# DeltaNet beside a streamed projection: keys turned one window ahead, key and query products as two jobs, TensorE's jobs placed by token half

## What is computed

```python
q, k, v = split(silu(causal_depthwise_conv(qkv, conv_w)))      # 4 taps
q, k = l2_normalize(heads(q)), l2_normalize(heads(k))
...
a_low = where(strict, einsum(k_beta, k) * gamma, 0)            # 64 x 64, per chunk of 64 tokens
u, w = triangular_solve(a_low + eye, [v * beta, k_beta * exp(decay)])
qk = einsum(q, k) * gamma
def step(state, inp):                                          # over the four chunks
    v_new = u_n - w_n @ state
    o_n = q_n @ state + qk_n @ v_new
    state = state * d_n + k_n.T @ v_new
o = rms_norm(o, norm_g) * silu(heads(z))
```

## Time and profile before

| | |
|---|---|
| median of 3 runs | 1931.12 us (1929.06 to 1935.96) |
| the profiled execution | 1928.9 us, its span 1927.1 us |
| granted TensorE clock, mean | 0.993 |
| busy: PE, PEld | 1875.4 us (97%), 1544.2 us (80%) |
| busy: DVE, ACT, POOL | 1100.5 (57%), 886.7 (46%), 130.9 us (7%) |
| DVE's split L1020, 584 times | 727.1 us, mean 1247 ns |
| ACT's split L673, 584 times | 618.8 us, mean 1061 ns |
| DMA | 316.37 MB, mean 164 GB/s |

### The profile page before, as it was taken

How to read it: one execution, slowest core, us unless ns; L and a number is a source line. 1 busy time by engine, 2 the same in 40 slices (tenths; PEclk the granted TensorE clock), 3 DMA queues, 4 the chain that set the end, 5 groups by cost and what they waited for, 6 DMA issues and landing times.

```text
span 1927.1 us, 29055 instructions
## 1 busy us (share of the span) xinstructions
PE 1875.4 (97%) x10770; PEld 1544.2 (80%) x10770; DVE 1100.5 (57%) x1441; ACT 886.7 (46%) x1384; POOL 130.9 (7%) x90
## 2 busy tenths in 40 slices
PE   7998998998999999999999999999999999999998
PEld 6877877877877888888888888888888888888886
DVE  5466576676676656666555555555544445555454
ACT  5453354353354355555444444444433344444443
POOL 0023023023023000000000000000000000000010
PEclk9999999999999999999999999999999999999999
DMA  7543333333333354444466655555555555555554
GB/s 255 173 143 115 116 121 121 110 123 118 111 121 121 110 170 141 153 152 141 163 196 199 205 197 208 186 185 177 191 191 193 196 186 188 185 185 193 191 193 142
DMA packets 88018, 316.37 MB, mean 164 GB/s; under 512 B 9712, under 2 KB 10224, under 8 KB 87792
## 3 DMA queue, kind: packets, MB, share of 16 engines
q1 hardware_dynamic: 87056, 312.65, 49.1%
q0 software_dynamic: 576, 2.10, 0.3%
q10 hardware_dynamic: 288, 0.18, 0.0%
HBM read 312.79 MB, written 2.10 MB: 163 GB/s over the span
## 4 chain that ended last, share of the span: by engine, by line
PE 89%; POOL 3%; DVE 3%; issue 3%; ACT 1%; DMA 0%; DVEq 0%; ACTq 0%; POOLq 0%; SPq 0%
PE acc L275 26%; PE acc L276 25%; PE acc L277 25%; PE J L398 4%; PE J L330 2%; PE J L446 1%; POOL rg L1455 1%; PE J L437 1%; PE J L454 1%; DVE cT L1075 1%; DVE qn L1075 1%; ACT w_hi L673 1%; PE J L489 1%; PE J L318 0%; POOL mats L1477 0%
## 5 line engine op out<-in xcount | busy, mean ns | idle before, releaser
L1020 DVE TENSOR_TENSOR w_lo<-raw,w_hi 128x1024 fp32r<-128x1024 f32 x584 | 727.1, 1247 | 635.2 <-ACT w_hi L673 633.6
L673 ACT ACTIVATE w_hi<-raw 128x1024 fp32r<-128x1024 f32 x584 | 618.8, 1061 | 684.2 <-PE acc L277 681.5
L275 PE MATMUL acc<-w_hi,hT_hi 128*128 128x512 f32 x1440 | 581.9, 404 | 8.4 <-DVE hT_lo L1038 4.3
L276 PE MATMUL acc<-w_lo,hT_hi 128*128 128x512 f32 x1440 | 564.2, 392 | 0.0
L277 PE MATMUL acc<-w_hi,hT_lo 128*128 128x512 f32 x1440 | 564.2, 392 | 0.0
L275 PEld LDWEIGHTS acc<-w_hi,hT_hi 128*128 128x128 f32 x1440 | 272.0, 189 | 71.2 <-issue 7.6
L277 PEld LDWEIGHTS acc<-w_hi,hT_lo 128*128 128x128 f32 x1440 | 272.0, 189 | 58.6
L276 PEld LDWEIGHTS acc<-w_lo,hT_hi 128*128 128x128 f32 x1440 | 272.5, 189 | 52.5 <-issue 1.0
L275 PE MATMUL acc<-w_hi,act_hi 128*128 128x512 f32 x512 | 199.3, 389 | 0.0
L277 PE MATMUL acc<-w_hi,act_lo 128*128 128x512 f32 x512 | 199.2, 389 | 0.0
L276 PE MATMUL acc<-w_lo,act_hi 128*128 128x512 f32 x512 | 199.2, 389 | 0.0
(11 more groups left out here) (224 smaller groups left out, 1498.4 us busy)
## 6 DMA issues: line engine op xcount, KB each, us to landing
raw<-weights SPq DMA_DIRECT2D x584, 512.0 KB, 3.3
xres<-x SPq DMA_DIRECT2D x4, 512.0 KB, 7.3
xres<-x POOLq DMA_DIRECT2D x4, 512.0 KB, 5.7
y<-nat SPq DMA_DIRECT2D x8, 256.0 KB, 3.1
fgain_sb<-fgain SPq DMA_DIRECT2D x1, 1024.0 KB, 6.9
masks_sb<-masks SPq DMA_DIRECT2D x1, 640.0 KB, 10.7
zs<-w_ba SPq DMA_DIRECT2D x1, 256.0 KB, 9.2
dist_sb<-dist SPq DMA_DIRECT2D x1, 192.0 KB, 3.5
```

Source lines behind the costliest of these rows:

```text
L275: mm(o, aT_hi[:, kt, tok], w_hi[:, c % RING, w], start=first, stop=False)
L276: mm(o, aT_hi[:, kt, tok], w_lo[:, c % RING, w], start=False, stop=False)
L673: A(w_hi[:, slot], raw[:, slot], ACT.Copy).then_inc(hi_ready, 1)
L1020: tt(w_lo[:, slot], raw[:, slot], w_hi[:, slot].bitcast(F32), ALU.subtract).then_inc(lo_ready, 1)
```

## The change

On PE the jobs are called after each token half's triple of products (`fine`), at places s = 0 to 127, with a table of its own; ACT and DVE keep 64 places with a table each. Raw K is turned 12 places before its window's end (`k_step`, called with s - 128 and h - 64 for the next group), and ACT's copies and the first tap follow there. Decay rows come before Q's front. Q's silu is written straight to `kq`, unnormalised, so that normalised Q isn't turned; Q's sum of squares enters as a term of the output's norm (`nq_done`). Key by key and key by query are two jobs (`inner`), at places 30 and 46. DVE makes the first X and U of the key product and ready masks; POOL makes those masks earlier. Z is not turned: its rows are evacuated with the two chunks of a tile exchanged, its silu is taken on them, and DVE's final scale takes it in (eight operations). After OT, ACT and DVE write `og_hi` and `og_lo` straight from PSUM. The diff, cut to its core:

```diff
-FRONT = {ITEM_K: 0, ITEM_Q: 1, ITEM_V: 25, ITEM_Z: 37}
-BANK = {ITEM_K: 0, ITEM_Q: 2, ITEM_V: 2, ITEM_Z: 2}
-TAPS = {ITEM_K: (0, 1, 2), ITEM_Q: (3, 5, 7), ITEM_V: (26, 28, 31)}
-TANH = {ITEM_K: 3, ITEM_Q: 9, ITEM_V: 32}
-SILU = {ITEM_K: 4, ITEM_Q: 10, ITEM_V: 33}
-BACK = {ITEM_K: 10, ITEM_Q: 16, ITEM_V: 34}
-NORM = {ITEM_K: 13, ITEM_Q: 19}
-ROWS, TK, TQ, KKQ, INV, QTM, OT = 11, 16, 21, 22, 25, 40, 63
-P1, P2, P3 = (40, 45, 50, 55), (42, 47, 52, 57), (44, 49, 54, None)
+BANK = {ITEM_K: 0, ITEM_Q: 2, ITEM_V: 2}
+PE_FRONT = {ITEM_K: -12, ITEM_Q: 19, ITEM_V: 56}
+PE_BACK = {ITEM_K: 16, ITEM_Q: 50, ITEM_V: 73}
+PE_ROWS, PE_TK, PE_KK, PE_KQ, PE_QT, PE_OT = 11, 28, 30, 46, 76, 126
+PE_INV_V = (46, 50, 55, 60, 69)
+PE_INV_U = (49, 52, 56, 66, 71)
+PE_P1, PE_P2, PE_P3 = (76, 85, 98, 109), (78, 92, 101, 112), (82, 96, 107, None)
+ACT_CONV = {ITEM_K: -4, ITEM_Q: 8, ITEM_V: 31}
+ACT_TANH = {ITEM_K: 5, ITEM_Q: 16, ITEM_V: 33}
+ACT_NSQ = {ITEM_K: 7, ITEM_Q: 27}
+ACT_EXP, ACT_NORM, ACT_KQ, ACT_Z, ACT_QT, ACT_OT = 6, 8, 13, 35, 38, 63
+ACT_INV = (21, 22, 27, 31, 33)
+ACT_VO = (40, 47, 49, 56)
+ACT_OSQ = (48, 59)
+DVE_CW, DVE_PAR = -17, 0
+DVE_TAPS = {ITEM_K: (-3, 0, 0), ITEM_Q: (8, 8, 16), ITEM_V: (31, 31, 31)}
+DVE_SILU = {ITEM_K: 5, ITEM_Q: 16, ITEM_V: 33}
+DVE_ROWS, DVE_NK, DVE_KQ, DVE_KK, DVE_EYE, DVE_KQM, DVE_NQ, DVE_VB, DVE_Z = 4, 7, 11, 14, 17, 19, 22, 35, 38
+DVE_INV = (21, 21, 24, 31, 34)
+DVE_RH, DVE_O, DVE_S = (37, 41, 49, 52), (38, 45, 49, 56), (38, 47, 52, None)
+DVE_OSUM, DVE_OSCALE, DVE_OT = 59, 59, 63
+STEPS, HALVES = 64, 128
...
                     for k in range(CK):
                         for t in range(NT):
                             last = product(par, t, aT_hi, aT_lo, c, k, c == 0 and k == 0, c == nch - 1 and k == CK - 1)
-                        if k == CK - 1:
-                            last.then_inc(chunk_used, 1)
+                            if k == CK - 1 and t == NT - 1:
+                                last.then_inc(chunk_used, 1)
+                            if fine:
+                                fine(NT * (h0 + c * CK + k) + t)
...
-            def gdn_step(h, g):
-                for n in range(4):
-                    if h == FRONT[n]:
-                        pe.wait_ge(rawg_a, 4 * g + (n + 1))
-                        if n == ITEM_K:
-                            pe.wait_ge(og_f, 2 * g + 2)
-                        if n == ITEM_V:
-                            pe.wait_ge(at_ready, g + 1)
-                        if n == ITEM_Z:
-                            pe.wait_ge(vb_done, g + 1)
-                        turn_group(rawg[:, n], BANK[n], front_T)
-                for n in (ITEM_K, ITEM_Q, ITEM_V):
-                    if h == BACK[n]:
-                        pe.wait_ge(silu_done, 4 * g + (n + 1))
-                        if n == ITEM_Q:
-                            pe.wait_ge(exp_done, g + 1)
-                        src = qnT if n == ITEM_Q else cT
-                        for t in range(NT):
-                            for m in range(HG):
-                                ins = tr(J[:, BANK[n] + t, m * P:(m + 1) * P], src[:, m, t * P:(t + 1) * P], ident)
-                        ins.then_inc(back_T, 1)
-                if h == TK or h == TQ:
-                    n = 0 if h == TK else 1
-                    pe.wait_ge(norm_done, 2 * g + (n + 1))
-                    src = qn if n else kn
+            def k_step(s, g):
+                if s == PE_FRONT[ITEM_K]:
+                    pe.wait_ge(rawg_a, 4 * g + 1)
+                    pe.wait_ge(rawg_d, 4 * g + 1)
+                    pe.wait_ge(o_done, NCH * g + NCH)
+                    turn_group(rawg[:, ITEM_K], BANK[ITEM_K], front_T)
+                if s == PE_BACK[ITEM_K]:
+                    pe.wait_ge(silu_done, 4 * g + 1)
                     for t in range(NT):
                         for m in range(HG):
-                            ins = tr(J[:, 2 * n + t, m * P:(m + 1) * P], src[:, t, m * P:(m + 1) * P], ident)
-                    ins.then_inc(qk_T, 1)
-                if h == ROWS:
+                            ins = tr(J[:, t, m * P:(m + 1) * P], cT[:, m, t * P:(t + 1) * P], ident)
+                    ins.then_inc(back_T, 1)
...
+            def inner(bank, other, done):
+                pe.sem_inc(step_begun, 1)
+                for u in range(U):
+                    t, hd = divmod(u, HG)
+                    for ck in range(2):
+                        c = 2 * t + ck
+                        kc = kq[:, hd, c * P + ck * C:c * P + ck * C + C]
+                        oc = kq[:, hd, c * P + (1 - ck) * C:c * P + (1 - ck) * C + C] if other else kc
+                        ins = mm(J[ck * C:ck * C + C, bank, u * C:(u + 1) * C], kc, oc, start=True, stop=True)
+                ins.then_inc(done, 1)
+            def gdn_step(s, g):
+                k_step(s, g)
+                if s == PE_ROWS:
                     pe.wait_ge(rows_rhs, 2 * g + 2)
-                    pe.wait_ge(conv_tap, 9 * g + 6)
+                    pe.wait_ge(og_lo_done, 2 * g + 2)
                     mm(J[:, 2], chunk_ones, mat(M_B0), start=True, stop=True)
                     mm(J[:, 3], chunk_ones, mat(M_B1), start=True, stop=True).then_inc(rows_done, 1)
-                if h == KKQ:
-                    pe.wait_ge(kq_a, 2 * g + 2)
+                if s == PE_TK:
+                    pe.wait_ge(norm_done, g + 1)
+                    for t in range(NT):
+                        for m in range(HG):
+                            ins = tr(J[:, t, m * P:(m + 1) * P], kn[:, t, m * P:(m + 1) * P], ident)
+                    ins.then_inc(qk_T, 1)
+                if s == PE_KK:
+                    pe.wait_ge(kq_a, g + 1)
                     pe.wait_ge(kq_d, g + 1)
-                    pe.sem_inc(step_begun, 1)
-                    for bank in range(2):
-                        for u in range(U):
-                            t, hd = divmod(u, HG)
-                            for ck in range(2):
-                                c = 2 * t + ck
-                                kc = kq[:, hd, c * P + ck * C:c * P + ck * C + C]
-                                qc = kq[:, hd, c * P + (1 - ck) * C:c * P + (1 - ck) * C + C]
-                                ins = mm(J[ck * C:ck * C + C, 2 + bank, u * C:(u + 1) * C], kc,
-                                         qc if bank else kc, start=True, stop=True)
-                    ins.then_inc(kkq_done, 1)
-                def per_chunk(bank, lhs, rhs, done):
-                    for u in range(U):
-                        for ck in range(2):
-                            r = slice(ck * C, ck * C + C)
-                            ins = mm(J[r, bank, u * C:(u + 1) * C], lhs[r, u], rhs[r, u], start=True, stop=True)
-                    if done is not None:
-                        ins.then_inc(done, 1)
+                    inner(0, False, kk_done)
+                if s == PE_FRONT[ITEM_Q]:
+                    pe.wait_ge(rawg_a, 4 * g + 2)
+                    pe.wait_ge(rawg_d, 4 * g + 2)
+                    pe.wait_ge(exp_done, g + 1)
+                    turn_group(rawg[:, ITEM_Q], 2, front_T)
+                if s == PE_KQ:
+                    pe.wait_ge(silu_done, 4 * g + 2)
+                    inner(3, True, kqp_done)
+                if s == PE_BACK[ITEM_Q]:
+                    pe.wait_ge(kqm_done, g + 1)
+                    for t in range(NT):
+                        for m in range(HG):
+                            ins = tr(J[:, 2 + t, m * P:(m + 1) * P], kq_q(m, t), ident)
+                    ins.then_inc(back_T, 1)
+                if s == PE_FRONT[ITEM_V]:
+                    pe.wait_ge(rawg_a, 4 * g + 3)
+                    pe.wait_ge(rawg_d, 4 * g + 3)
+                    pe.wait_ge(nsq_done, 2 * g + 2)
+                    turn_group(rawg[:, ITEM_V], 2, front_T)
...
                 for lv in range(LEVELS):
-                    if h == INV + 3 * lv:
+                    if s == PE_INV_V[lv]:
                         pe.wait_ge(bt_ready, LEVELS * g + (lv + 1))
                         if lv:
                             pe.wait_ge(inv_done, LEVELS * g + lv)
                         else:
-                            pe.wait_ge(x0_ready, g + 1)
+                            pe.wait_ge(u0_ready, g + 1)
                         pe.sem_inc(step_begun, 1)
                         per_chunk(0, mat(M_B0 + lv % 2), mat(M_X), vpass)
-                    if h == INV + 3 * lv + 1:
+                    if s == PE_INV_U[lv]:
                         pe.wait_ge(vcopy, LEVELS * g + (lv + 1))
-                        if lv == 0:
-                            pe.wait_ge(u0_ready, 2 * g + 2)
                         pe.sem_inc(step_begun, 1)
                         per_chunk(1, mat(M_U), mat(M_V), None)
                         per_chunk(0, mat(M_V), mat(M_U), zpass)
-                if h == QTM:
+                if s == PE_QT:
                     pe.wait_ge(inv_done, LEVELS * (g + 1))
```

(80 more changed lines are left out.)

348 lines of the change are left out of this document (194 added, 154 removed).

## The result

The changed kernel takes 1878.04 us, the median of 4 runs (1877.38 to 1878.71), beside 1931.08 for the kernel before on the same chip: a ratio of 0.9725, 95% interval 0.9707 to 0.9743. That is 53.0 us less where 45 were forecast, at the very low end of the range.

What follows compares the result with a forecast made beforehand. TensorE's in-order queue was taken as the bound: 42.4 us of stalls plus 5.8 of removed work less 4 of new stalls takes 44.2 off the profiled 1928.9, giving 1884.7; with part of the runs' offset, 1886 us, range 1878 to 1906.

Steps and rivals of the forecast that it cites:

- The bound: Whole kernel: TensorE busy 97% of the span, its in-order queue sets the time; its waits are for a chain, not throughput.
- The stalls, 42.4 us: Four DeltaNet windows: waits at decay rows, turned K, turned Q and first inversion pass, with its clock drop, go: 42.4 us.
- Removed PE work, 5.8 us: PE per group: two sets of transposes (Z, normalised Q) fewer, one changeover of 0.3 more; net 1.4 x 4 = 5.8 us.
- The count of places: New windows: PE's arrival at each place against its input's readiness; nine places have slack under 0.5 us.
- New stalls, 4 us off the gain: Nine tight places in the new windows: 1.0 us a window taken between bounds 0 and 4, so 4 us lost.
- The loop's edge is as before: PE at the loop's edge: nothing changes there, so no gain or loss was counted.
- The rule on ports: DVE splits during POOL's masks: exclusive port lock makes them up to 2.29 us against 1.23; 0.5 us extra counted.
- The lock's rival: Mask phase: every split 1.06 us longer, key product 2.8 us late each window, about 1896 us; chance 0.15.
- The low end of my range: Whole kernel: 1880.7 us with no new stall, and a run's scatter below that: 1878 us.
- Half lost: Nine tight places each 0.7 us late, or one stop halves the clock: gain 26 us, 1905 us; chance 0.09.
- not what it says: The chain simply waits elsewhere for as long, only the 5.8 us of removed work remain: 1925 us; chance 0.01.
- slower: DVE late at some 16 places where PE waits; decides from 1.3 us each, 1995 us at 2.29; chance 0.03.

Runs made afterwards that it cites:

- k_own: Changed kernel with K's front (transposes, ACT's copies, first tap) at the start of its own window as before: 1884.37 us.
- the two kernels: Changed kernel with the key product moved next to the first pass, 1892.68 us; and with the first X made on POOL again, distance kept, 1877.25 us.
- b_places: Kernel before with only its table of places changed, most jobs one to three places later: 1904.95 us beside 1928.86, ratio 0.987.
- dve_busy: Changed kernel with one more DVE operation of 1.22 us per group ahead of the recurrence's third Rh, result unused: 1880.78 us.
- the merged jobs: Changed kernel with Q's front at place 16, V's turn back at 71 and the output's transposes at 124: 1880.19 us.
- kk_late: Changed kernel with the key product at place 45, next to the key-query product at 46, DVE's masked products behind it: 1892.68 us.

## Why the prediction was right or wrong

*The bound.* Right. PE's queue set the time, the waits were for a chain, and with them gone PE is busy 99% of the span. An extra set of transposes costs its full price.

*The stalls, 42.4 us.* Right in size. All four groups of waits vanished, and with them the low clock behind the first pass and, in two windows, behind Q's turn. That K's lead matters is shown by k_own; that the decay rows no longer wait for Q's taps is read from the trace only. For the first pass I named both DVE's part and the place; the two kernels show that it is the place alone. And by b_places the table alone ends all four groups, if not without new waits; leaving Q's norm to the output is worth its eight transposes.

*Removed PE work, 5.8 us.* Right, a little low. A set costs its 0.88 or 0.89 by experiment. The split of the 64 matmuls, which I took at 0.3, cost 0.15: key-query product and first pass stand at one place, 46, and share one changeover. That makes 6.5 us.

*The count of places.* This held best. For the tight ones the slack forecast and the idle margin found in the changed trace, second window of the loop, in us: turn back of K at 16, 0.4 and 0.6; K turn at 28, 1.7 and 2.2; key product at 30, 0.4 and 0.6; first pass at 46, 1.1 and 2.1; V at 50, 0 and 0.4; V at 55, 0.8 and 0.9; P2 at 78, 0.1 and 0.2; P1 at 98, 0.3 and 0.3; P2 at 101, 0 and 0.4; P1 at 109, 0.3 and 0.3. For place 50, for instance, these are DVE's two subtractions, the second ending at 288.94, and PE's pass, which starts at 289.31:

```profile
287.65 0.69 DVE L1219 TENSOR_TENSOR mats<-mats,J 128x512 f32<-128x512 f32 x1 [3.46 <-PE J L385]
288.26 0.68 DVE L1222 TENSOR_TENSOR mats<-mats,J 128x512 f32<-128x512 f32 x1
```

```profile
289.31 0.80 PE L385 MATMUL J<-mats 64*64 64x64 f32 x20
```

*New stalls, 4 us off the gain.* **This is the first step that failed.** The count showed no link late, and I still charged 1.0 us a window for its own inaccuracy. There was none to pay: PE's list of waits has no job of the windows in it. My errors went to the safe side throughout: each wait was counted with a hop, and several durations at their slow value (the power at 2.71 in the earlier trace rows took 1.64 in the new place).

*"The loop's edge is as before".* **The second.** I put this term at nothing without a reason. The two stops at the branch fell by 1.4 and 1.1 us of idle time, 2.5 together. And at the entry of the last stretch a wait of its K front for the old output (0.5 us idle) and one for a chunk split late (0.4) went away, 0.7 us each by the starts of the products around them; both stood in the list of waits before. Against these 3.9 us the part ahead of the windows grew by 1.4 us beyond its K front. 44.2 + 4 + 0.7 (removed work) + 2.5 + 1.4 - 1.4 = 51.4, which is the difference of the spans (1927.1 - 1875.7; the times differ by 51.1). The low end of my range, no new stall and nothing else, had no room for a gain outside the count; the median fell on its edge.

*The rule on ports.* The lock's rival didn't happen. While POOL makes its masks ahead of the key product, DVE's splits now take 1.2 us each, two of them 2.35 together:

```profile
251.05 2.35 DVE L1099 TENSOR_TENSOR w_lo<-raw,w_hi 128x1024 fp32r<-128x1024 f32 x2
...
268.24 2.35 DVE L1099 TENSOR_TENSOR w_lo<-raw,w_hi 128x1024 fp32r<-128x1024 f32 x2
```

Most of POOL's masks now fall into DVE's waits and into its PSUM operations, and where the two meet POOL is longer: its scaling of K takes 2.90 us, where it took 1.89 in the kernel before, and DVE's split that meets it and the level mask before it takes 1.96. That is the one split in each window that is still long (1.56 to 1.96); before there were three to five (1.47 to 2.29).

```profile
272.96 1.96 DVE L1099 TENSOR_TENSOR w_lo<-raw,w_hi 128x1024 fp32r<-128x1024 f32 x1
```

```profile
272.52 1.31 POOL L1597 TENSOR_TENSOR mats<-mats,masks_sb 128x512 f32<-128x512 f32 x1
273.77 2.90 POOL L1601 TENSOR_TENSOR kn<-kn,scg 128x1024 f32<-128x1024 f32 x1
```

That either side can be the one that is held is what the Trainium skill's page SBUF — State Buffer says in Who interferes with whom: whoever issues first has the ports. The trace agrees, with 2.29 for DVE before, and 1.96 for DVE and 2.90 for POOL after. Nobody waits for that K before place 82, so it costs nothing.

*Half lost, not what it says, slower.* None came. The slower one needed PE's sixteen waits to be late by 1.3 us each; by dve_busy a single lateness of 1.22 costs 0.7 at its place and nothing behind it.

## What to carry to other kernels

Where one in-order engine is the bound and a dependent chain is laid into its stream, write down for each job when the engine reaches it and when its input is ready; that count, made from the trace's durations, was good to 0.6 us at all but one of ten places, though it doesn't replace the run: the merged jobs were expected to gain a little, and they lost 2 us. Moving a producer away from its consumer is what pays, and much of it can be had by the table alone (24 of 53 us here); which engine does the step between, and how fine the places are, mattered less than a microsecond. A stop of 2 to 3 us on TensorE can cost more than itself, since the clock was at half behind some of them: in kk_late behind two of four, for some 1.5 us each on top of the 10.1 us of idle time, and in the kernel before for 2.7 behind the first pass of the earlier trace rows.

## What the runs showed that I had not expected

The stop of PE at a loop's branch isn't a constant of the loop: it is 1.4 to 2.3 us of idle time in kernels that turn a group's K in its own window, 0.5 to 1.05 in those that turn it a window ahead, and neither the job ahead of the branch nor the distance of the one behind it changes that. In every one PE goes on 2.7 to 3.2 us after the start of a 16 KB instruction transfer; that this transfer is what it stands for is likely, but not settled. And the kernel before scatters more than the changed one: its medians in four sets of runs were 1926.8, 1931.3, 1928.9 and 1934.3, while each of the changed kernels keeps within 3 us in its four runs apart from kk_late, which has long stops and low clock as the kernel before does. The times go with the mean granted clock: the kernel before took 1926.8 us at 0.994 and 1936.0 at 0.987, kk_late 1891.0 at 0.997 and 1897.7 at 0.992. That fits a scatter in how many stops the low clock follows; what decides that at a given stop, these runs don't show.
